# The samples' query rows spread over partitions by TensorE into PSUM instead of through DRAM

## What is computed

```python
def cross_attention(x, k, v, g, wq, wo):
    B, S, _ = x.shape
    h = rms_norm(x, g)
    q = (h @ wq).reshape(B, S, XA_HEADS, XA_HEAD_DIM)            # 4 heads of 256
    s = jnp.einsum('bshd,bmhd->bhsm', q, k) * (XA_HEAD_DIM ** -0.5)
    p = jax.nn.softmax(s, axis=-1)
    o = jnp.einsum('bhsm,bmhd->bshd', p, v).reshape(B, S, D_MODEL)
    return o.astype(x.dtype) @ wo
```

## Time and profile before

| | |
|---|---|
| median of 3 runs | 1234.06 us (1231.25 to 1236.54) |
| the profiled execution: its span, first to last instruction | 1234.4 us |
| PE busy | 1169.4 us, 95% of the span |
| DVE busy | 591.4 us, 48% |
| ACT busy | 420.4 us, 34% |
| mean granted clock of TensorE | 0.965 of full speed |
| the chain that ended last | PE 89%, DVE 4%, DMA 4%, ACT 1%, issue 1% |

### The profile page before, as it was taken

The page is one execution under the profiler, slowest core; times in us unless marked ns, Lnnn a source line. Parts: engine busy times, 40 slices in busy tenths (PEclk is TensorE's granted clock), DMA queues, the critical chain, the costliest instruction groups (busy, mean ns, idle before and its releaser), DMA issues.

```text
span 1234.4 us, 16784 instructions
## 1 busy us (share of the span) xinstructions
PE 1169.4 (95%) x5584; PEld 756.5 (61%) x5584; DVE 591.4 (48%) x1394; ACT 420.4 (34%) x654; POOL 190.5 (15%) x180
## 2 busy tenths in 40 slices
PE   6999999898899998999999999999999999999991
PEld 5996579895369885455555555555555555555551
DVE  5734454527514333254555555555545555455552
ACT  4373343325512111233333333333332333333333
POOL 1003200000000101022222222212222122221220
PEclk7999999898999699899999999999999999999996
DMA  9403331608641514399999999999999999999934
GB/s 312 161 1 148 136 141 66 273 1 297 250 155 61 214 62 165 108 327 330 339 328 335 336 337 330 330 339 340 338 336 325 334 344 341 337 334 326 336 100 155
DMA packets 65605, 303.22 MB, mean 246 GB/s; under 512 B 12824, under 2 KB 15460, under 8 KB 40983
## 3 DMA queue, kind: packets, MB, share of 16 engines
q1 hardware_dynamic: 50254, 266.15, 57.2%
q0 software_dynamic: 15312, 36.55, 12.0%
HBM read 285.92 MB, written 34.04 MB: 259 GB/s over the span
## 4 chain that ended last, share of the span: by engine, by line
PE 89%; DVE 4%; DMA 4%; ACT 1%; issue 1%; SPq 0%; DVEq 0%; POOLq 0%
PE pair L1735 36%; PE pair L171 16%; PE pair L1755 14%; PE pair L1723 4%; PE pair L1525 4%; PE pair L1429 3%; PE pair L1631 2%; DMA regA<-q_rows 2%; PE pair L1683 1%; PE pair L1650 1%; DVE regL L1041 1%; PE pair L1744 1%; PE pS L1699 1%; DMA regA<-in_w_in 1%; DMA acc_rows<-regL 1%
## 5 line engine op out<-in xcount | busy, mean ns | idle before, releaser
L1735 PE MATMUL pair<-regA,regL 128*96 128x512 f32 x512 | 235.3, 603 | 3.0 <-DVE regL L1360 3.0
L1755 PE MATMUL pair<-down_parts,act_parts 128*96 128x512 f32 x768 | 192.0, 399 | 1.2 <-DVE act_parts L1375 1.2
L686 POOL DMA_INDIRECT acc_rows<-regL x64 | 94.9, 1483 | 524.2 <-DVE regL L1251 337.0
L1755 PEld LDWEIGHTS pair<-down_parts,act_parts 128*96 128x96 f32 x768 | 121.2, 164 | 46.1 <-DVE act_parts L1375 1.3
L1735 PEld LDWEIGHTS pair<-regA,regL 128*96 128x96 f32 x512 | 80.5, 167 | 108.4 <-issue 108.4
L171 PE MATMUL pair<-h_hi,w_parts 128*128 128x260 f32 x640 | 131.0, 286 | 3.9 <-DVE h_lo L1035 3.5
L1735 PE MATMUL pair<-regC,regL 128*96 128x512 f32 x256 | 116.0, 596 | 0.0
L1735 PE MATMUL pair<-regB,regL 128*96 128x512 f32 x256 | 116.0, 596 | 0.0
L171 PEld LDWEIGHTS pair<-h_hi,w_parts 128*128 128x128 f32 x640 | 104.2, 191 | 4.8 <-issue 3.0
L1381 DVE TENSOR_SCALAR regL<-pair,regL 96x512 f32<-96x512 f32 x64 | 47.8, 747 | 118.0 <-PE pair L1755 118.0
L1371 DVE TENSOR_TENSOR down_parts<-regB,down_parts 128x2048 fp32r<-128x2048 f32 x32 | 73.3, 2292 | 43.9 <-ACT down_parts L966 43.9
(11 more groups left out here) (306 smaller groups left out, 1626.2 us busy)
## 6 DMA issues: line engine op xcount, KB each, us to landing
regA<-in_exp_w_gate SPq DMA_DIRECT2D x32, 1024.0 KB, 10.0
regA<-in_exp_w_up SPq DMA_DIRECT2D x32, 1024.0 KB, 14.9
regA<-in_exp_w_down SPq DMA_DIRECT2D x32, 1024.0 KB, 9.3
regB<-in_exp_w_down SPq DMA_DIRECT2D x32, 1024.0 KB, 9.3
regB<-in_exp_w_gate SPq DMA_DIRECT2D x16, 1024.0 KB, 10.0
regB<-in_exp_w_up SPq DMA_DIRECT2D x16, 1024.0 KB, 14.9
regC<-in_exp_w_gate SPq DMA_DIRECT2D x16, 1024.0 KB, 10.1
regC<-in_exp_w_up SPq DMA_DIRECT2D x16, 1024.0 KB, 15.1
```

The costliest lines, as they stand in the source:

```text
L686: pool.indirect_dma_start(acc_rows, bass.IndirectOffsetOnAxis(ap=sidx[0:SLOTS, r:r + 1].bitcast(U32), axis=0), yX[r][0:SLOTS, :], None, bo ...
L1735: ins = pe.matmul(pair[0][0:SLOTS, 0, :].rearrange("p (s f) -> p s f", s=2), hX[:, k, :], w[:, :, k, :], start=k == 0, stop=k == KD - 1, s ...
L1755: ins = pe.matmul(pair[2][0:SLOTS, h, :], act_parts[:, x, k, :], down_parts[r % PAIR][:, w, k, h * 512:(h + 1) * 512], start=k == 0 and s ...
```

## The change

The query rows of the samples no longer go to DRAM. PE's product `qs` is cut into two parts in SBUF: ACT copies it rounded to `float32r` (`qs_parts[:, 0]`), DVE subtracts that from the product (`qs_parts[:, 1]`), so that the two add up to the full value; `qs` is now given back by DVE. A small matrix `pick` holds the 8 x 8 identity. For each sample and each half of the heads PE multiplies one column of `pick`, repeated 128 times, with the two parts (`spread_query`, two matmuls of 8 x 512): all 128 partitions of one bank of `pS` then hold 512 numbers of the sample's query. DVE reads the query from there. A call `scores(b, half)` is again four instructions, now for two heads and both memory tiles, made in step n for unit n-1, from n = 1 on.

SP's list changes with it: keys 4, 5 and values 0 to 3 are started when the last `q` product is made, keys 6 and 7 when the first and the second sample are scored.

```diff
@@ product_order
-    o += [(("q", m), "act") for m in range(KD)] + [("qs", "act")]
+    o += [(("q", m), "act") for m in range(KD)] + [("qs", "dve")]
@@ sync
-            J.wait_taken(sp, "qs")
-            sp.dma_start(q_rows, qsr[0:DEC, :]).then_inc(q_stored, 16)
-            sp.wait_ge(q_stored, 16)
-
-            sp.wait_ge(stored, 16 * 8)
-            for b in range(DEC):
-                if b >= 2:
-                    sp.wait_ge(qb_used, b - 1)
-                sp.dma_start(qb[:, b % 2, :], q_rows[b, :].partition_broadcast(P)).then_inc(qb_in[b % 2], 16)
-                if b == 1:
-                    for j in (4, 5):
-                        sp.dma_start(kcache[j], ck[:, j]).then_inc(kc_in[j - 4], 16)
-                if b in (2, 3):
-                    sp.dma_start(kcache[b + 4], ck[:, b + 4]).then_inc(kc_in[b], 16)
-                if b >= 4:
-                    sp.dma_start(vc[b - 4], cv[:, b - 4]).then_inc(v_in[1], 16)
-            sp.wait_ge(qb_used, DEC)
+            sp.wait_ge(made, J.no[("q", KD - 1)] + 1)
+            for b in (4, 5):
+                sp.dma_start(kcache[b], ck[:, b]).then_inc(kc_in[b - 4], 16)
+            for b in range(4):
+                sp.dma_start(vc[b], cv[:, b]).then_inc(v_in[1], 16)
+            for b in (6, 7):
+                sp.wait_ge(qb_used, 2 * (b - 6) + 2)
+                sp.dma_start(kcache[b], ck[:, b]).then_inc(kc_in[b - 4], 16)
+            sp.wait_ge(qb_used, 2 * DEC)
@@ scalar
             p = J.wait_made(a, "qs")
-            J.take(a.copy(qsr[0:DEC, :].rearrange("p (h n) -> p h n", h=2), pair[p][0:DEC, :, :]), "qs")
+            a.wait_ge(stored, 16 * 8)
+            a.copy(qs_parts[0:DEC, 0, :].rearrange("p (h n) -> p h n", h=2), pair[p][0:DEC, :, :]).then_inc(qs_hi, 1)
@@ vector
-            def scores(b, mt):
-                if mt == 0:
-                    v.wait_ge(qb_in[b % 2], 16 * (b // 2 + 1))
+            def scores(b, half):
+                v.wait_ge(qb_made, 2 * b + half + 1)
+                if half == 0:
                     if b < 4:
                         v.wait_ge(kb_in, 64)
                     else:
                         v.wait_ge(kc_in[b - 4], 16)
-                for h in range(HEADS):
-                    kk = kcache[b][:, mt, h * HD:(h + 1) * HD]
-                    ins = v.tensor_tensor_reduce(kk, kk, qb[:, b % 2, h * HD:(h + 1) * HD], 1.0, 0.0, ALU.mult, ALU.add,
-                                                 sS[:, mt, h * DEC + b:h * DEC + b + 1])
-                if mt == MT - 1:
-                    ins.then_inc(qb_used, 1)
+                for mt in range(MT):
+                    for i in range(2):
+                        h = 2 * half + i
+                        kk = kcache[b][:, mt, h * HD:(h + 1) * HD]
+                        ins = v.tensor_tensor_reduce(kk, kk, pS[:, half, i * HD:(i + 1) * HD], 1.0, 0.0, ALU.mult, ALU.add,
+                                                     sS[:, mt, h * DEC + b:h * DEC + b + 1])
+                ins.then_inc(qb_used, 1)
@@ vector, ahead of the loop
             v.wait_ge(stored, 16 * 8)
             v.memset(pad8, 0.0)
+            v.tensor_copy(pick[0:DEC, :], ident[0:DEC, 0:DEC])
+            p = J.wait_made(v, "qs")
+            v.wait_ge(qs_hi, 1)
+            J.take(v.tensor_tensor(qs_parts[0:DEC, 1, :].rearrange("p (h n) -> p h n", h=2), pair[p][0:DEC, :, :],
+                                   qs_parts[0:DEC, 0, :].bitcast(F32).rearrange("p (h n) -> p h n", h=2), ALU.subtract), "qs")
@@ vector, in the loop
-                if n >= 2:
-                    for u in range(n - 2, n - 1 if n < len(STEPS) else len(units)):
-                        scores(*units[u])
+                if n >= 1:
+                    scores((n - 1) // 2, (n - 1) % 2)
@@ tensor
+            def spread_query(b, half):
+                if b:
+                    pe.wait_ge(qb_used, 2 * b + half - 1)
+                for x in range(2):
+                    ins = pe.matmul(pS[:, half, :], pick[0:DEC, b:b + 1].to_broadcast((DEC, P)),
+                                    qs_parts[0:DEC, x, half * 512:(half + 1) * 512], start=x == 0, stop=x == 1)
+                ins.then_inc(qb_made, 1)
+
@@ tensor, in the loop, behind the scores s of step n
+                    if n == 1:
+                        J.wait_taken(pe, "qs")
+                        spread_query(0, 0)
+                        spread_query(0, 1)
+                    elif n >= 2:
+                        spread_query(n // 2, n % 2)
```

More of the change, by code:

```diff
@@ L234, in trunk @@
             pass
+        with nc.sbuf_tensor("unused_A2", [P, 8192], F32), nc.sbuf_tensor("qs_parts", [P, 2, D], F32R) as qs_parts:
+            pass
         regA = sb("regA", [P, 12288])
@@ L253, in trunk @@
         small = sb("small", [P, 160])
+        pick = sb("pick", [P, DEC], F32R)
         def view(reg, at, *shape):
@@ L318, in trunk @@
         vspare = [view(regL, 10304, MT, D), view(regL, 12352, MT, D)]
-        qb = view(regA, 8192, 2, D)
         pr = view(regA, 10240, 4, NMEM)
@@ L324, in trunk @@
         oSr = view(regL, 4160, D)
-        qsr = view(regL, 5184, D)
         oT, o_lo = hT, h_hi
@@ L412, in trunk @@
         stored = sem("stored")
-        q_stored, qb_in, qb_used = sem("q_stored"), [sem("qb_in0"), sem("qb_in1")], sem("qb_used")
+        qs_hi, qb_made, qb_used = sem("qs_hi"), sem("qb_made"), sem("qb_used")
         kc_in, kb_in, v_in = [sem(f"kc_in{b}") for b in range(4, DEC)], sem("kb_in"), [sem(f"v_in{j}") for j in range(3)]
@@ L858, in _ @@
             p = J.wait_made(a, "qs")
-            J.take(a.copy(qsr[0:DEC, :].rearrange("p (h n) -> p h n", h=2), pair[p][0:DEC, :, :]), "qs")
+            a.wait_ge(stored, 16 * 8)
+            a.copy(qs_parts[0:DEC, 0, :].rearrange("p (h n) -> p h n", h=2), pair[p][0:DEC, :, :]).then_inc(qs_hi, 1)
             nb = DEC * HEADS
-            a.wait_ge(stored, 16 * 8)
             def out(h, cc):
@@ L882, in _ @@
                     h, t = STEPS[n - BEHIND]
-                    if (h, t) == (1, 0):
-                        a.wait_ge(q_stored, 16)
                     q = J.wait_made(a, ("pT", h, t))
@@ L899, in _ @@
             J.take(a.copy(pad8[:, :, 0:DEC * DEC:DEC + 1], bank[q][:, 0:MT * nb].rearrange("p (g b) -> p g b", b=DEC)), "pS")
-            a.wait_ge(qb_used, DEC)
+            a.wait_ge(qb_used, 2 * DEC)
             J.wait_taken(a, ("o", HEADS - 1, 1))
@@ L1179, in _ @@
                 Q.cut_lo(v, u)
-            units = [(b, mt) for b in range(DEC) for mt in range(MT)]
-            def scores(b, mt):
-                if mt == 0:
-                    v.wait_ge(qb_in[b % 2], 16 * (b // 2 + 1))
+            def scores(b, half):
+                v.wait_ge(qb_made, 2 * b + half + 1)
+                if half == 0:
                     if b < 4:
@@ L1611, in _ @@
             q = J.begin(pe, "sS")
-            pe.wait_ge(qb_used, DEC)
+            pe.wait_ge(qb_used, 2 * DEC)
             for m in range(MT):
```

## The result

The changed kernel takes **1249.88 us** (median of 4 runs, 1247.81 to 1251.0), the kernel before 1235.3 on the same chip (1231.25 to 1236.6). The ratio is 1.0125, with a 95% interval of 1.0105 to 1.0145: slower by 1.25%, some 15 us. The forecast was 1236.8, and its range ended at 1241.0: the measured time lies 8.9 us above the range. The profiled execution of after took 1251.0 us, with a span of 1249.3, beside the 1234.4 of before; so the traces differ by 14.9 us.

What follows compares the result with a forecast made beforehand. The change was taken to matter only through when `oS` starts, a line of untouched matmuls following. Parts 1 to 4 gave +0.9 us, the early clock fall +1.8; with +2.7, 1234.06 became 1236.8 us, range 1231.5 to 1241.0.

Steps and rivals of the forecast that it cites:

- part 5: Clock at the attention's start: falls to half in a 2.4 us PE idle time, low 3.4 to 6.8 us, costing 1.8 us.
- Rival (c): Slower: low clock lasts into the output products, a pair takes 8.9 us, +3.3 each; 1243 to 1250 us; chance 0.08.
- Part 1: Start of the attention: first scores at 284.5 instead of 286.21, a gain of 1.7 us, despite DVE's added subtraction.
- Part 2: Steps without output product: PE needs 1.55 us, below DVE's 1.96, so DVE keeps its pace; unit 6 ends at 297.6.
- Part 3: Steps with an output product: the spread's wait ties the engines into a line, 5.6 us per two steps; unit 14 ends 320.0.
- Part 4: Tail from the last reciprocal to `oS`: 7.5 us instead of 8.9, so `oS` starts at 327.5, +0.9 us.
- Part 6: Transfers: q_rows store and eight broadcasts go; all eight loads landed by 306, with 6 us of room.
- The query in PSUM: Score instructions reading one operand from PSUM: taken to cost 0, between ends of 0 and 0.06 us for each of 64.
- rival (b): A PSUM operand costs 0.06 us per score instruction, +2.6 us in all; 1237.6 to 1240.1 us; chance 0.16.
- Rival (d): Faster: the handshake does not bind, PE's 4.85 us a pair sets the pace; 1228.3 to 1232 us; chance 0.06.

Runs made afterwards that it cites:

- e1_dup: Changed kernel with the scores of step 1 computed twice and of step 2 three times, filling TensorE's idle time at the start; 1236.72 us, stretch 49.68 us.
- e4_late: Changed kernel with each spread behind the transposes and output product of its step instead of ahead; 1246.53 us, stretch 59.34 us.
- e2_rows128: Changed kernel with each spread matmul contracting over 128 rows instead of 8, `qs_parts` placed in `w_parts`; 1239.66 us, stretch 49.89 us.
- e6_tied: e1_dup with the cache loads (keys 6, 7, values 0 to 3) again issued behind a sample's scores; 1237.39 us, stretch 49.68 us.
- e8_best: Changed kernel with one 128-row matmul per spread, spreads last, repeated start scores, eight unread matmuls ahead of `x2`; 1231.95 us in one run, stretch 43.64 us.
- e5_nospread: Changed kernel with only the first sample's two spreads, every sample scored with that query; 1229.33 us, stretch 41.32 us.
- e8_timed: e8_best again, timed: 1230.56 us (12 runs) beside 1234.45 for the kernel before, ratio 0.9974.
- e10_best_nodup: e8_best without the repeated score matmuls at the start; 1232.24 us in one run.
- e10_timed: e10_best_nodup again, timed: 1231.42 us (10 runs) beside 1233.35 for the kernel before, ratio 0.9981; stretch 44.38 us.
- e3_hi_only: Changed kernel with one 8-row matmul per spread instead of two, the query's lower part left out of the scores; 1242.76 us, stretch 56.43 us.
- e2_alias: Control of e2_rows128: changed kernel with `qs_parts` placed in `w_parts`, spreads still over 8 rows; 1250.91 us, stretch 60.87 us.
- e11_shift1: Changed kernel with its query transposes issued twice, so all that follows comes later; 1254.22 us, stretch 61.18 us.
- e11_shift2: Changed kernel with its query transposes issued three times, so all that follows comes later; 1250.63 us, stretch 60.97 us.

## Why the prediction was wrong

**The step that failed is part 5, the length of the low clock.** I expected the fall, at about the right idle time (2.4 us predicted, 1.82 measured) and the right place. I took it to last 3.4 us and at most 6.8, the two lengths of before, and chose the short one "since PE would be busy throughout". PE was busy throughout from 286.58 on, and it lasted 27 us. Both low stretches of before ended over work of 128-row matmuls, in output products. I carried their length over to steps with a spread over 8 rows in each, and no step of before has such a matmul, so nothing in the trace supported that length. The term was 1.8 us; it measured 10.9 (60.56 of after less 49.68 of e1_dup).

**Rival (c) was the nearest**, with a chance of 0.08 and 1243 to 1250 us. Its mechanism, low clock lasting into the output products, happened, but in another proportion. Only one pair ran at half clock, 8.40 us (8.9 predicted); most of the cost, 8.3 of 10.9 us, lies in the light steps ahead of it. The argument that I put against it, PE busy nearly all the time, was no argument.

The other steps, by e1_dup, which is the changed kernel at full clock, and by after:

- **Part 1, the start: right.** First scores at 285.07 in after, 5.13 us behind the first score matmul; predicted 284.5, 5.2 behind. The subtraction took 1.21 us (1.2).
- **Part 2, the light steps: the pace nearly right, PE's work too small.** A step took 2.02 us at full clock (1.96). But PE's share was 1.89 (318.15 to 320.04 in after; 1.93 in e4_late), not 1.55, and that made half clock dearer: 3.47 a step, not 3.1. A spread stood 0.65 us ahead of the next matmul, not 0.47, `s` 0.96 ahead of the spread, not 0.86, and `pT` 0.28, not 0.22. This, too, comes with the 8 rows: e2_rows128 has the same matmuls in the same order, its spreads over 128 rows, and `s`, spread and `pT` took the predicted 1.55 (303.31 - 301.76; timeline of PE in e2_rows128):

```profile
301.76 1.03 PE L1598 MATMUL pair<-regA,regL 128*128 128x256 f32 x4
302.44 0.82 PE L1589 MATMUL pS<-w_parts,pick 128*128 128x512 f32 x2
303.09 0.38 PE L1612 MATMUL pair<-ident,regA 128*128 128x128 f32 x2
303.31 1.03 PE L1598 MATMUL pair<-regA,regL 128*128 128x256 f32 x4
```

  PEld, the weight load, stood idle on "issue" ahead of the 8-row spreads in after, and in no place ahead of the 128-row ones. That the 8-row loads don't overlap with the matmuls ahead of them is my reading of this, which no run tests by itself (after; engine, line, waited for, total, times, longest):

```profile
PEld pS L1590 <- issue: 5.2, 10, 0.7
```

- **Part 3, the pairs: the mechanism right, the size 0.2 short.** 321.31 - 315.50 = 5.81 us (5.6), with PE waiting 0.24 for DVE at the head of each pair at full clock. The cleanest case is e2_rows128: PE's work is the predicted one, and a pair takes 5.65 (304.92 to 310.57), of which PE waits 0.58 for DVE. So the handshake gives the 5.6. e4_late shows that PE's own work with 8-row spreads holds a pair at 5.58 as well.
- **Part 4, the tail: right.** It took 7.7 us, from the last reciprocal at 332.77 to `oS` (7.5). At full clock the stretch is 2.4 us longer than before (49.68 against 47.32), where parts 1 to 4 gave 0.9: the four pairs make 0.8 of the difference, seven light steps 0.4.
- **Part 6, the transfers: right.** DVE never waited for a load, the DMA share ends near 301.3 (306 predicted), and e6_tied has the same stretch as e1_dup.
- **The query in PSUM: right, rival (b) is out.** Groups of DVE instructions by line and shape (count, busy us, mean ns, idle), after first, then before:

```profile
L1184 DVE CUSTOM_DVE_ANT_0 regB<-regB,pS 128x256 f32<-128x256 f32 x48 | 17.1, 412 | 0.0
```
```profile
L1193 DVE CUSTOM_DVE_ANT_0 regB<-regB,regA 128x256 f32<-128x256 f32 x48 | 17.4, 418 | 6.5 <-DMA regA<-q_rows 6.5
```

  412 ns with the query in PSUM, 418 with it in SBUF. The Trainium skill's overhead of some 60 ns on SBUF and 125 ns on PSUM ("Perfetto Trace Analysis", section "Optimizing Scalar/DVE Operations") is not borne out here for an instruction with one of two tensors in PSUM.
- **Rival (d), faster, was right about where the gain could be**, but not for this kernel: the pair of 4.34 us came only with e8_best, whose spread is one matmul over 128 rows behind the step's other work. (d) had 4.85.
- **Outside the stretch** I expected nothing. In after the clock fell once more at the head of `x2`:

```profile
370.00:372.00 2.00, 1.16 (x7) 1.07 (x6) 0.23 (x1) 0.46 (x2) 0.00 (x0) 0.64 0.65 106
372.00:374.00 2.00, 2.00 (x11) 2.00 (x11) 0.00 (x0) 0.00 (x0) 0.00 (x0) 0.50 0.83 261
```

  The work there is the same in all kernels, with 1.18 and 0.84 us idle ahead. By the busy time of `x2`'s 256 `o_hi` matmuls, 46.1 us or 47.3 to 47.6, the clock fell in ten of the twelve kernels that keep these idle times, e5_nospread among them, and not before and not in e4_late. So neither the change nor these idle times force this fall; whether the change makes it likelier, one trace of before can't tell. With the idle times filled they took 46.1 in all four traces (e8_best, e8_timed, e10_best_nodup, e10_timed). The price is 1.3 us.

## What to carry to other kernels

Ask of a new idle time on TensorE two things: whether the clock can fall in it, and which matmuls stand behind it to lift it again; here one or two matmuls over 8 rows in every step went with a busy engine that stayed at half speed. Filling the gap with repeated matmuls, or giving the narrow matmul its full 128 rows, took back 11 us of 13. Where a handshake and an engine's own work bound a loop at the same height, test the two edits together: each alone took 0.2 us off a pair, both together, with the spread over 128 rows, 1.5 (5.81 to 4.34).

## What the runs showed of the hardware

- In steps with matmuls that contract over 8 rows the granted clock did not come back: it stayed at 0.50 for 27 us with PE busy nearly throughout (after), for 23.9 us with half as many of them (e3_hi_only), but only for 3.4 us with 128 rows (e2_rows128, and e10_timed with one such matmul a step). At full clock the same 8-row matmuls did not lower it (e1_dup). Whether it is the rows in use, the weight loads or something else that goes with them, no run here separates.
- The fall and the idle time are not tied to one distance: the clock fell 0.5 us after the start of the idle time in after, and 1.4 us after its end in e2_rows128 (idle to 286.10, low from 287.54).
- Whether the clock falls after an idle time differs between executions of one program (e10_best_nodup and e10_timed, 2.61 us idle). At the head of `x2`, 1.18 and 0.84 us idle, it differs between kernels with the same work there. In the kernels with the 8-row spreads and 1.8 to 2.3 us idle it fell in every trace taken (after, e2_alias, e3_hi_only, e4_late, e11_shift1, e11_shift2). What decides it stays open.
- The same matmuls of a step at full clock (`s`, spread, `pT`) took PE 1.89 us with the two spread matmuls over 8 rows (after) and 1.55 us with them over 128 rows (e2_rows128).
